# A relative-position bias built by one product of eight columns, and unread products at two block boundaries

## What is computed

```
def rel_bucket(q_pos, k_pos):
    max_exact = REL_BUCKETS // 2
    n = jnp.maximum(q_pos - k_pos, 0)
    ...
    return jnp.where(n < max_exact, n, large)

# in diff_attention (bias_a = rel_bias[:, :4]); dsa_attention does the same with rel_bias[:, 4:]
bias = bias_a[rel_bucket(q_pos[:, None], k_pos[None, :])].transpose(2, 0, 1)
s = s * A_SCALE + bias[None, :, None].astype(jnp.float32)
```

## Time and profile before

| | us |
|---|---|
| median of three runs | 2149.15 |
| span of the profiled execution, first to last instruction | 2143.4 |
| what lies around the span (median less span) | 5.75 |
| TensorE busy | 2108.3 |
| VectorE busy | 1477.1 |
| ScalarE busy | 1017.9 |
| GpSimd busy | 481.6 |
| loads issued by SyncE, share of the 16 DMA engines | 49.4% |

### The profile page before, as it was taken

One profiled execution on the slowest core, in us unless ns is written; L12 is line 12 of the kernel. 1 busy time (PEld: TensorE's weight loads), 2 busy tenths in 40 slices (PEclk: granted clock), 3 DMA queues, 4 the chain that ended last, 5 costly groups with the idle time before them and its releaser, 6 DMA issues.

```text
span 2143.4 us, 43268 instructions
## 1 busy us (share of the span) xinstructions
PE 2108.3 (98%) x16240; PEld 1928.0 (90%) x16240; DVE 1477.1 (69%) x2517; ACT 1017.9 (47%) x1377; POOL 481.6 (22%) x518
## 2 busy tenths in 40 slices
PE   8999999999999999999999999999999999999999
PEld 7997779989999888799889987799889998779998
DVE  7884778857688667688678846788565546586553
ACT  4335765544455443555443346655453334364332
POOL 3220005510135314044212200054113300201320
PEclk9999999999999999999999999999999999999999
DMA  6555235565645644245645553255645556305554
GB/s 189 187 178 185 89 125 177 193 201 181 206 144 189 208 155 148 69 158 193 205 160 182 190 179 117 83 183 190 204 150 173 171 182 187 99 21 177 185 180 145
DMA packets 300950, 350.37 MB, mean 163 GB/s; under 512 B 7604, under 2 KB 255990, under 8 KB 300854
## 3 DMA queue, kind: packets, MB, share of 16 engines
q1 hardware_dynamic: 296358, 344.75, 49.4%
q10 hardware_dynamic: 4112, 4.07, 0.6%
q0 software_dynamic: 384, 0.24, 0.0%
HBM read 346.35 MB, written 2.68 MB: 163 GB/s over the span
## 4 chain that ended last, share of the span: by engine, by line
PE 90%; DVE 4%; ACT 4%; issue 1%; ACTq 0%; DVEq 0%
PE ps L2312 26%; PE ps L2314 26%; PE ps L2313 26%; PE ps L2741 2%; DVE w_lo L1693 1%; ACT w_hi L1263 1%; PE ps L2449 1%; PE ps L2444 1%; PE ps L2445 1%; ACT prob L566 1%; PE ps L2678 1%; PE ps L2381 1%; PE ps L2691 1%; PE ps L2324 1%; PE ps L2290 0%
## 5 line engine op out<-in xcount | busy, mean ns | idle before, releaser
L1693 DVE TENSOR_TENSOR w_lo<-raw,w_hi 128x2048 fp32r<-128x2048 f32 (+3 forms) x310 | 694.0, 2239 | 452.9 <-ACT w_hi L1263 452.7
L2312 PE MATMUL ps<-a_hi,w_hi 128*128 128x256 f32 (+1 forms) x3200 | 906.2, 283 | 6.2 <-DVE w_lo L1702 2.7
L2314 PE MATMUL ps<-a_hi,w_lo 128*128 128x256 f32 (+1 forms) x3200 | 903.3, 282 | 0.0
L2313 PE MATMUL ps<-a_lo,w_hi 128*128 128x256 f32 (+1 forms) x3200 | 903.1, 282 | 0.0
L1263 ACT CAST w_hi<-raw 128x2048 fp32r<-128x2048 f32 (+3 forms) x318 | 587.4, 1847 | 542.2 <-PE ps L2314 528.5
L2312 PEld LDWEIGHTS ps<-a_hi,w_hi 128*128 128x128 f32 x3200 | 604.8, 189 | 12.8 <-issue 5.8
L2314 PEld LDWEIGHTS ps<-a_hi,w_lo 128*128 128x128 f32 x3200 | 605.5, 189 | 0.0
L2313 PEld LDWEIGHTS ps<-a_lo,w_hi 128*128 128x128 f32 x3200 | 602.5, 188 | 0.4 <-issue 0.2
L2217 POOL TENSOR_TENSOR hs<-sg,cv 128x256 f32<-128x256 f32 x88 | 65.5, 744 | 642.6 <-DVE cv L2054 642.6
L2224 POOL CAST hid_hi<-hs 128x256 f32 (+3 forms) x132 | 137.8, 1044 | 297.0 <-DVE hs L2100 282.7
L2312 PE MATMUL ps<-w_hi,hid_hi 128*128 128x512 f32 x480 | 189.5, 395 | 2.3 <-DVE w_lo L1689 1.2
(11 more groups left out here) (359 smaller groups left out, 2552.5 us busy)
## 6 DMA issues: line engine op xcount, KB each, us to landing
raw<-in_ffn_w_in_dram SPq DMA_DIRECT2D x88, 1024.0 KB, 5.1
raw<-in_attn_w_qkv_dram SPq DMA_DIRECT2D x71, 1024.0 KB, 5.1
raw<-in_ffn_w_out_dram SPq DMA_DIRECT2D x32, 1024.0 KB, 5.0
raw<-in_ffn_w_gate_dram SPq DMA_DIRECT2D x22, 1024.0 KB, 5.3
raw<-in_ffn_w_up_dram SPq DMA_DIRECT2D x22, 1024.0 KB, 5.3
raw<-in_ffn_w_down_dram SPq DMA_DIRECT2D x16, 896.0 KB, 4.8
raw<-in_sc_w_in_dram SPq DMA_DIRECT2D x12, 1024.0 KB, 5.1
raw<-in_ffn_w_out_dram SPq DMA_DIRECT2D x16, 768.0 KB, 4.5
```

The lines of the kernel that those rows point to most:

```text
L1693: dve.tensor_tensor(o, src, hi.bitcast(F32), ALU.subtract).then_inc(lo_ready, 1)
L2312: pe.matmul(o, wh, xh, start=start, stop=False)
L2313: pe.matmul(o, wh, xl, start=False, stop=False)
L2314: return pe.matmul(o, wl, xh, start=False, stop=stop)
```

## The change

The eight columns of the table become one product: `relb` (33 x 8) against `hot` gives 8 x 399, one row for each head, in bank 2, at the first boundary alone. ScalarE copies these eight rows once. The transfer to the scratch tensor reads each of the eight partitions 128 times, by a source pattern with a repeated dimension, and writes the same bytes to the same places as the two transfers did. `relw` and its eight VectorE operations go away, the second boundary has nothing of the bias, and one semaphore `skew_stored` takes the place of two. The first boundary gets two unread products and then the one more; the second gets five and one, as the others have.

```
-        skew_stage = put("skew_stage", [P, N_BIAS, SKEW], R_Q + 14 * D + D // 2)
+        skew_stage = put("skew_stage", [N_BIAS, SKEW], R_Q + 14 * D + D // 2)
-        relw = put("relw", [BUCKETS + 1, N_BIAS, P], R_Q + 10 * D + D // 4)
...
         def rel_sums(pe, ph):
-            if ph in gaps:
-                pe.wait_ge(relw_ready, 1)
+            if ph is rel_gap:
+                pe.wait_ge(rel_landed, 16)
                 pe.wait_ge(hot_landed, 16)
-                for k in rel_heads[gaps.index(ph)]:
-                    pe.matmul(ps[:, k % 4, 0:SKEW - 1], relw[:, k, :], hot[:, 0:SKEW - 1],
-                              start=True, stop=True).then_inc(rel_done, 1)
+                pe.matmul(ps[0:N_BIAS, 2, 0:SKEW - 1], relb, hot[:, 0:SKEW - 1], start=True, stop=True).then_inc(rel_done, 1)
 
         def rel_copies(act, ph):
-            if ph in gaps:
-                for k in rel_heads[gaps.index(ph)]:
-                    act.wait_ge(rel_done, k + 1)
-                    act.copy(skew_stage[:, k, 0:SKEW - 1], ps[:, k % 4, 0:SKEW - 1]).then_inc(skew_ready, 1)
-                heads = rel_heads[gaps.index(ph)]
-                act.wait_ge(skew_ready, heads[-1] + 1)
-                act.dma_start(scratch[:, heads[0]:heads[-1] + 1, 0:SKEW - 1],
-                              skew_stage[:, heads[0]:heads[-1] + 1, 0:SKEW - 1]
-                              ).then_inc(skew_stored[gaps.index(ph)], 16)
+            if ph is rel_gap:
+                act.wait_ge(rel_done, 1)
+                act.copy(skew_stage[:, 0:SKEW - 1], ps[0:N_BIAS, 2, 0:SKEW - 1]).then_inc(skew_ready, 1)
+                act.wait_ge(skew_ready, 1)
+                act.dma_start(scratch[:, :, 0:SKEW - 1].rearrange("p h i -> h p i"),
+                              skew_stage[:, 0:SKEW - 1].rearrange("h (a i) -> h a i", a=1).to_broadcast([N_BIAS, P, SKEW - 1])
+                              ).then_inc(skew_stored, 16)
...
                 elif ph.kind == "out":
-                    if ph is rel_phase:
-
-                        dve.wait_ge(hid_ready, B["hid"])
-                        dve.wait_ge(rel_landed, 16)
-                        for k in range(N_BIAS):
-                            op = dve.tensor_scalar(relw[:, k, :], ones[0:BUCKETS + 1, :], relb[:, k:k + 1], None, ALU.mult)
-                        op.then_inc(relw_ready, 1)
-
...
-                        if n and pre.prior not in gaps:
+                        if n:
                             for _ in range(count):
                                 pe.matmul(ps[:, 3, :], identb[:], maskb[:, 0:512], start=True, stop=True)
...
-                            keep_on(5)
+                            keep_on(2 if pre.prior is rel_gap else 5)
...
-                        if n and pre.prior in gaps:
-                            pe.wait_ge(skew_ready, rel_heads[gaps.index(pre.prior)][-1] + 1)
+                        if n and pre.prior is rel_gap:
+                            pe.wait_ge(skew_ready, 1)
```

## The result

The changed kernel takes 2165.08 us (median, 2162.18 to 2170.74), the kernel before beside it 2148.83 us (2147.18 to 2150.51). The ratio is 1.0076, with a 95% interval of 1.0064 to 1.0087: slower by 16.3 us, where 8.0 were forecast. The span of the profiled execution is 2163.5 us.

A forecast was written before the change was run, and what follows sets the result against it. TensorE, busy 98% of the span, was taken as the bound, so only its standstills count. Profiled span 2143.4 - 3.9 gained + 11.8 for the transfer = 2151.3 us; median 2157.1, 0.37% slower, range 2144.0 to 2162.0.

The forecast's parts named there:

- Gains: Out phase without `relw` 0.88 us, second boundary 1.45, first boundary 1.60: 3.93 us saved in all.
- Copy, issue and one product at no cost: At the first boundary, ScalarE's copy and issue fit an idle stretch of 1.07 us; at most 0.9 us if late.
- Rate of the transfer: Transfer to scratch from eight partitions on eight engines: 67 ns a packet at best, 268 at worst; the latter was taken.
- the worst case: In the transfer, four neighbouring partitions share one way out of memory: 268 ns a packet, 34.3 us.
- The port estimate: Skill page's 27.6 GB/s for partitions 0 to 3: transfer 30 us, delay 8 to 13 us, time 2154 to 2158.
- both queues move equal bytes: Transfer and loads share eight engines by bytes: 11.8 us cost; 0.48 together with sharing by whole packets.
- load A: First of three loads after the first boundary, wanted by ScalarE at 315.9 us; forecast to land at 321.6, 5.7 late.
- turns of whole packets: Transfer and loads alternate packet by packet on shared engines: up to 16.4 us late, time 2161.7.
- Hidden transfer: Rival: eight engines keep 24 GB/s each or 16 serve; 8.6 us transfer fits before the loads, 2145.2 us; chance 0.36.
- Loads pass it: Rival: transfer is long but engines serve loads meanwhile, or two share the way; cost 0 to 8 us; chance 0.12.
- The change gives no gain: Rival: time saved without `relw` and at the boundaries is taken by the next waits; 2149 us; chance 0.04.

The follow-up runs named there:

- e4_early_relw: Kernel before, with only the eight `relw` operations moved from the head of the out phase to the first attention's value phase: 2148.58 us, ratio 1.0003.
- e1_step4: Changed kernel with the eight rows on partitions 0, 4, ... 28 instead of 0 to 7: 2143.33 us, ratio 0.998 to the kernel before.
- e5_step16: Changed kernel with the eight rows on partitions 0, 16, ... 112: 2152.29 us, 3.8 us over the kernel before.
- e10_filled_more: Changed kernel with 84 unread products put on TensorE where it stands still before the late load: 2166.96 us, of only four executions.
- e6_rows64: Changed kernel with 64 of the 128 repeats written and the skewed read in two parts: 2150.52 us, 2.0 us over the kernel before.
- e7_rows96: Changed kernel with 96 of the 128 repeats written and the skewed read in parts of 96 and 32 rows: 2158.67 us.
- e9_doubled: Changed kernel with rows on partitions 0, 16, ... 112, each repeated 256 times instead of 128, the second half unread: 2158.43 us.
- e2_wide: Changed kernel with all 128 rows made by the product, each head 16 times, each partition repeated eight times: 2144.29 us, ratio 0.9982.
- e3_rows32: Changed kernel with 32 of the 128 repeats written and the skewed read in parts of 32 rows: 2143.76 us, 4.4 us less than before.
- e8_filled_wait: Changed kernel with 72 unread products put on TensorE where it stands still before the late load: 2165.23 us.

## Why the prediction was wrong, point by point

- **Gains: right.** `relw` 0.88 forecast, 0.89 in the changed kernel, and in the same stretch of e4_early_relw. Second boundary 1.45 forecast, 1.47 by the windows. First boundary 1.71 by the windows, for which 1.60 was taken. The sum of 3.93 is best seen where the transfer costs nothing: e1_step4 has 2.46 + 0.07 + 1.43 = 3.96 in the three stretches, and -4.8 in the medians (-2.4 to -6.2 by the interval).
- **Copy, issue and one product at no cost: right.** ScalarE still waits 0.69 us behind them.
- **Rate of the transfer: right, a little too slow.** 268 ns a packet came from four neighbours on one way; 234 was measured. e1_step4 and e5_step16 show that this is the cause, and neither the number of engines nor the reading of one partition many times. But the argument by which I chose the worst case does not hold: that a partition gave 3 GB/s in the old rows does not show that it can't give more, and in e1_step4 one gave 22. So far as it rests on that, the choice was luck. The port estimate beside it had the transfer nearly right (30 us, measured 33); its delay of 8 to 13 us fell with the rule for sharing.
- **The failed step: "I therefore take it that both queues move equal bytes."** With it load A was to be 5.7 us late, B 11.2 and C 11.8; by turns of whole packets the most was 16.4. Both rules assumed that sharing begins at once. In fact A's part on the shared engines waits for some 50 packets of the transfer (13.3 us), and only then come turns, one for one. With A's last packet near 334 us in place of 314.4, TensorE waits 18.90 us in one piece, at A; B and C come in time after that. The row behind the rule was one fetch of instructions that took longer beside loads. It can't show how long a newcomer waits before its first turn, since it was not behind a queue of slow packets.
- **A term that was missing: the clock after the wait.** I gave a fallen clock no share, and thought of it only at the boundary. It fell because TensorE stood still: 2.7 us by the windows, 2.4 by e10_filled_more. It costs much the same after the waits of 4 to 19 us here. The stretch less the wait is 7.68 - 5.06 = 2.6 in e5_step16, 1.8 in e6_rows64, 2.9 in e7_rows96, 2.2 in e9_doubled, 2.6 in the changed kernel.
- **The sum.** Forecast -3.9 + 11.8 = +7.9. Found in the trace: -4.1 + 18.9 + 2.6 = +17.4, with +16.3 in the timed medians. Of the 9.5 us between the two sums, 7.1 are the order of the queues (less what the shorter packets give back), 2.6 the clock, and the gains take 0.2 back.
- **The rivals.** *Hidden transfer* was a real one: e1_step4, e2_wide and e3_rows32 show no loss behind the first boundary, and come out 3.8 to 4.8 us under before, where that rival gave 3.9. What decided was which partitions the rows lie on, and that was not settled by the rows that I had. *Loads pass it* is the opposite of what happened. *The change gives no gain* fell too: e1_step4 keeps 3.96 us.

## What to carry to other kernels

When a small tensor is sent out many times, put eight rows four partitions apart (0, 4, ... 28), or repeat them over all 128: a product's zero columns cost nothing here, and the same transfer went from 33 us to 9 and 6. Price a long transfer not by its share of the traffic but by the first load that comes behind it on the same engines, which here waited for some 50 of its packets; so it should be over before that load, and if it can't be, shorter packets make the wait shorter (10.7 us in e9_doubled, 18.9 in the changed kernel). To a long wait of TensorE add the lower clock that followed it, here 1.8 to 2.9 us after waits of 4.4 to 18.9 us.

## What the runs showed of the hardware that I had not expected

- A load that arrived on engines busy with another queue's transfer got no packet through for about 50 packets of that transfer, at 234 ns as at 127 ns, and then one for each of them.
- Once the turns had begun in e9_doubled, a packet of the transfer took 88 ns in place of 127, so its queue still moved 7.7 packets a us on each engine, against 7.9 before (127 ns a packet).
- SyncE's issue of load B took 2.35 us in place of 0.38 in the changed kernel, while A was held up, and 2.35 or 2.36 in e6_rows64, e7_rows96, e8_filled_wait and e10_filled_more, all with packets of 234 ns. In e5_step16 and e9_doubled, where A was held up too but by packets of 127 ns, it took 0.38, as in e1_step4. Why is not tested. It lies on no path here.

```profile
312.01 2.35 SPq L1176 DMA_DIRECT2D raw<-in_ffn_w_in_dram  x1
```

- The length of a wait alone does not tell whether TensorE's granted clock falls. It fell within one of 3.23 us in e8_filled_wait and stayed at 1.00 through 0.67 us in e10_filled_more, but it also fell in e4_early_relw with a wait of 0.86 us, and did not in e10_filled_more at one of 2.3 us near 1116 us.
